# Latent attention's head linears from FP32 matmuls to three passes on split weights

## The reference

```python
def _mla_queries(a_q, q_a_norm, w_uq, q_norm, rope):
    q = (_rms_norm(a_q, q_a_norm) @ w_uq).reshape(B, L, MLA_HEADS, QK_HEAD_DIM)   # 16 heads of 96
    q = _rms_norm(q, q_norm)
    # rope on the last 32 of 96
def _mla_keys_values(a_kv, kv_a_norm, w_ukv, k_norm, rope):
    ckv = _rms_norm(a_kv[..., :KV_LORA_RANK], kv_a_norm)
    kv = (ckv @ w_ukv).reshape(B, L, MLA_HEADS, QK_NOPE_DIM + V_HEAD_DIM)         # 64 + 64
    # keys: 64 columns of kv beside 32 shared rope columns, normed, rope
```

## Time and profile before

| | |
|---|---|
| median of 3 runs | 3414.77 us (3411.88 to 3416.74) |
| span of the profiled execution | 3412.4 us; no time beside the span is recorded for it |
| TensorE busy | 3261.6 us, 96% |
| VectorE, ScalarE, GpSimd busy | 42%, 38%, 41% |
| latent attention: prologue from the first query tile to the first scores | 1044.4 to 1075.8 us |
| its 64 items, first to last scores | from 1075.8 to about 1330 us |
| items 16 to 32 by their exponentials | 1142.63 to 1216.13, 73.5 us |

### The profile page before, as it was taken

How to read it: one execution, slowest core, us unless ns; L and a number is a source line. 1 busy time by engine, 2 the same in 40 slices (tenths; PEclk the granted TensorE clock), 3 DMA queues, 4 the chain that set the end, 5 groups by cost and what they waited for, 6 DMA issues and landing times.

```text
span 3412.4 us, 40303 instructions
## 1 busy us (share of the span) xinstructions
PE 3261.6 (96%) x16296; PEld 2583.0 (76%) x16296; DVE 1418.5 (42%) x2558; ACT 1307.4 (38%) x2311; POOL 1393.8 (41%) x788
## 2 busy tenths in 40 slices
PE   7989999999999889999999999999999999999998
PEld 4864788888875456788886688888887768878887
DVE  5556342222246664321222757243232658434132
ACT  4221342212235666432333534353333443444243
POOL 2223432322343334444463036544455215554445
PEclk9989999999999999999999999999999999999999
DMA  6134223121222000423232021332323111122322
GB/s 229 62 115 180 103 86 130 56 74 45 63 83 85 13 13 10 141 84 112 84 115 99 19 79 28 104 104 84 109 86 118 51 43 60 43 90 90 108 84 71
DMA packets 85638, 286.08 MB, mean 84 GB/s; under 512 B 9771, under 2 KB 10347, under 8 KB 84940
## 3 DMA queue, kind: packets, MB, share of 16 engines
q1 hardware_dynamic: 85452, 283.50, 25.4%
HBM read 281.37 MB, written 2.10 MB: 83 GB/s over the span
## 4 chain that ended last, share of the span: by engine, by line
PE 87%; DVE 7%; ACT 4%; DMA 1%; issue 1%; POOL 0%; SPq 0%; DVEq 0%; ACTq 0%
PE ps L459 20%; PE ps L462 20%; PE ps L460 20%; PE ps L1999 2%; PE ps L499 2%; PE ps L501 2%; PE ps L500 2%; PE ps L529 1%; DMA ring<-in_w_mod 1%; PE ps L2069 1%; PE ps L1226 1%; PE ps L437 1%; PE ps L2043 1%; PE ps L2394 1%; PE ps L438 1%
## 5 line engine op out<-in xcount | busy, mean ns | idle before, releaser
L411 POOL TENSOR_TENSOR WL<-ring,WH 128x1024 fp32r<-128x1024 f32 (+2 forms) x443 | 961.4, 2174 | 1520.3 <-ACT WH L402 1519.9
L459 PE MATMUL ps<-HX,WH 128*128 128x512 f32 x1768 | 695.4, 393 | 3.0 <-POOL WL L411 3.0
L462 PE MATMUL ps<-HX,WL 128*128 128x512 f32 x1768 | 692.4, 392 | 0.0
L460 PE MATMUL ps<-HX,WH 128*128 128x512 f32 x1768 | 690.5, 391 | 0.0
L402 ACT CAST WH<-ring 128x1024 fp32r<-128x1024 f32 (+2 forms) x443 | 420.2, 950 | 371.0 <-PE ps L462 312.9
L459 PE MATMUL ps<-FR,WH 128*128 128x512 f32 x1120 | 419.1, 374 | 0.3
L460 PE MATMUL ps<-FR,WH 128*128 128x512 f32 x1120 | 409.7, 373 | 0.0
L459 PEld LDWEIGHTS ps<-HX,WH 128*128 128x128 f32 x1768 | 332.5, 188 | 82.5 <-issue 7.4
L462 PE MATMUL ps<-FR,WL 128*128 128x512 f32 x1120 | 389.4, 373 | 0.0
L462 PEld LDWEIGHTS ps<-HX,WL 128*128 128x128 f32 x1768 | 333.6, 189 | 49.9
L460 PEld LDWEIGHTS ps<-HX,WH 128*128 128x128 f32 x1768 | 332.8, 188 | 49.0
(11 more groups left out here) (391 smaller groups left out, 5096.7 us busy)
## 6 DMA issues: line engine op xcount, KB each, us to landing
ring<-in_w_mod SPq DMA_DIRECT2D x96, 512.0 KB, 5.5
ring<-in_ffn_w_up SPq DMA_DIRECT2D x88, 512.0 KB, 3.4
ring<-in_w_up SPq DMA_DIRECT2D x88, 512.0 KB, 3.3
ring<-in_w_in_tok SPq DMA_DIRECT2D x40, 512.0 KB, 3.4
ring<-in_w_in_feat SPq DMA_DIRECT2D x32, 512.0 KB, 3.3
ring<-in_ffn_w_down SPq DMA_DIRECT2D x32, 384.0 KB, 3.1
ring<-in_w_out SPq DMA_DIRECT2D x32, 384.0 KB, 3.2
ring<-in_w_down SPq DMA_DIRECT2D x32, 384.0 KB, 3.1
```

What stands on the lines that cost most here:

```text
L411: pool.tensor_tensor(WL[:, p % SPLITS, 0:n], ring.ap(r), WH[:, p % SPLITS, 0:n], ALU.subtract).then_inc(*ring.frees(r, split.g, "low", p))
L459: pe.matmul(o, high, xh, first, False)
L460: pe.matmul(o, high, xl, False, False)
L462: m = pe.matmul(PS[bs[i]][:, 0:N], low, get(k)[0], False, last)
```

## The change

The head linears join the common sequence as `L_h`, eight weights between `L_a` and `L_o`, and run in three passes. Their input gets a low part: ScalarE writes the high part in fp32r, VectorE subtracts it from the result in PSUM, and the bank is now released by VectorE. `LOW` needs room for the low parts behind the old slab, so `ARENA` grows by 1792 words; the room is taken from the scratch of dynamic transfers. ScalarE casts one weight after the last query tile and one after the last key tile of each group, three ahead in the sequence; GpSimd makes the remainders at steps 3 and 8. The three weights prepared ahead of attention are now those of group 0 and the queries of group 1, and the `L_o` weights are prepared in groups 2 and 3.

```diff
-ARENA = 27200
+ARENA = 28992
...
+        LOW = [nc.alloc_sbuf_tensor_at(f"LOW{x}", [128, 1792], F32R, offset=base + 4 * at) for x, at in enumerate((0, 27200))]
...
         L_a = Linear(ring, "mla_a").rows(dr["mla_w_a"], 0, 3, 8)
+        L_h = Linear(ring, "heads")
+        for n_ in range(4):
+            L_h.group(("q", n_), [(dr["mla_w_uq"][n_], 768, 0, 2)])
+            L_h.group(("kv", n_), [(dr["mla_w_ukv"][n_], 512, 0, 1)])
         L_o = Linear(ring, "mla_o").rows(dr["mla_w_o"], 0, 8, 8)
...
-        aq = buf(0, 2, 512)
-        ckv = buf(1024, 768)
+        aq = [x[:, 0:1024].rearrange("p (a b) -> p a b", a=2) for x in LOW]
+        ckv = [x[:, 1024:1792] for x in LOW]
...
-                    act.activation(dst, o, ACT.Identity, scale=gain).then_inc(*bank.emptied((L_a.name, g.key, s), mla.a))
+                    act.activation(low_rank_of(0, g.key, s), o, ACT.Identity, scale=gain).then_inc(
+                        *mla.a.up("rank", g.key, s))
...
+            for g in L_a.groups:
+                gain = col("mla_q_a_norm", g.key) if g.key < 2 else col("mla_kv_a_norm", 0)
+                for s in range(1 + (g.key == 2)):
+                    dve.wait_ge(*mla.a.at("rank", g.key, s))
+                    dve.scalar_tensor_tensor(low_rank_of(1, g.key, s), ps(L_a.name, g.key, s)[:, 0:(S, SC)[s]], gain,
+                                             low_rank_of(0, g.key, s), ALU.mult, ALU.subtract).then_inc(
+                        *bank.emptied((L_a.name, g.key, s), mla.v, "rank", g.key, s))
...
+        def heads_tile_pe(pe, n, what, t, x, N):
+            g = heads_of(n, what)
+            p = g.last
+            b = bank.take(what, n, t)
+            pe.wait_ge(*bank.free(what, n, t))
+            for k in range(g.kt):
+                high, low = WH[:, p % SPLITS, k * N:k * N + N], WL[:, p % SPLITS, k * N:k * N + N]
+                xh, xl = (y[:, k, t * 128:t * 128 + 128] for y in x)
+                pe.matmul(PS[b][:, 0:N], xh, high, k == 0, False)
+                pe.matmul(PS[b][:, 0:N], xh, low, False, False)
+                m = pe.matmul(PS[b][:, 0:N], xl, high, False, k == g.kt - 1)
+            m.then_inc(*(split.pe.up("used", p) if t == {"q": 3, "kv": 5}[what] else mla.pe.up(what, n, t)))
...
         def heads_pe(pe, n):
-            r = ring.raw(dr["mla_w_uq"][n], 768)
-            pe.wait_ge(*ring.landed(r))
...
+            for what, x, N, tiles in (("q", aq, 384, 4), ("kv", [y.unsqueeze(1) for y in ckv], 512, 6)):
+                p = heads_of(n, what).last
+                assert ring.next() == p
+                pe.wait_ge(*split.g.at("low", p))
...
         def heads_a(act, n):
...
                 act.copy(qtok[:, t, :], ps("q", n, t)[:, 0:384]).then_inc(*bank.emptied(("q", n, t), mla.a, "q", n, t))
+                if t == 3:
+                    cast_to(act, heads_of(n, "q").last + 3)
...
+                if t == 5:
+                    cast_to(act, heads_of(n, "kv").last + 3)
...
         def heads_g(pool, n):
             for step in range(15):
                 if step in (1, 2, 5, 6, 7):
                     square_g(pool, n, step - 1 if step < 3 else step - 3)
+                if step == 3:
+                    rest_to(pool, heads_of(n, "q").last + 3)
+                elif step == 8:
+                    rest_to(pool, heads_of(n, "kv").last + 3)
                 yield
...
-    nc = _bacc.Bacc("TRN2", target_bir_lowering=False, num_devices=1)
+    nc = _bacc.Bacc("TRN2", target_bir_lowering=False, num_devices=1, dynamic_dma_scratch_size=1024)
```

More of the change, by code:

```diff
@@ L1694, in low_rank_pe, with low_rank_of @@
             m.then_inc(*mla.pe.up("kpe"))
+        def low_rank_of(x, key, s):
+            return aq[x][:, key, :] if key < 2 else ckv[x][:, 0:512] if s == 0 else ckv[x][:, 512:768]
         def low_rank_a(act):
@@ L1703, in low_rank_a @@
                     o = ps(L_a.name, g.key, s)[:, 0:N]
-                    dst = aq[:, g.key, :] if g.key < 2 else ckv[:, 0:512] if s == 0 else ckv[:, 512:768]
                     act.activation(sq[:, g.key + s, 0:N], o, ACT.Square).then_inc(*mla.a.up())
-                    act.activation(dst, o, ACT.Identity, scale=gain).then_inc(*bank.emptied((L_a.name, g.key, s), mla.a))
+                    act.activation(low_rank_of(0, g.key, s), o, ACT.Identity, scale=gain).then_inc(
+                        *mla.a.up("rank", g.key, s))
                 mla.a.mark("low")
@@ L1797, in squares_of @@
             return s[:, 0:8 * w].rearrange("p (a b) -> p a b", a=8)
-        def heads_pe(pe, n):
-            pe.wait_ge(*mla.a.at("low"))
-            r = ring.raw(dr["mla_w_uq"][n], 768)
-            pe.wait_ge(*ring.landed(r))
[L1803 to L1828, removed]
@@ new lines, in heads_of, with done_of @@
+        def heads_of(n, what):
+            g, = (g for g in L_h.groups if g.key == (what, n))
+            return g
+        def done_of(n, what, t):
+            return split.pe.at("used", heads_of(n, what).last) if t == {"q": 3, "kv": 5}[what] else mla.pe.at(what, n, t)
+        def heads_tile_pe(pe, n, what, t, x, N):
[10 more added lines that the diff above has]
+            m.then_inc(*(split.pe.up("used", p) if t == {"q": 3, "kv": 5}[what] else mla.pe.up(what, n, t)))
@@ new lines, in heads_pe @@
+        def heads_pe(pe, n):
+            for what, x, N, tiles in (("q", aq, 384, 4), ("kv", [y.unsqueeze(1) for y in ckv], 512, 6)):
+                p = heads_of(n, what).last
+                assert ring.next() == p
+                pe.wait_ge(*split.g.at("low", p))
+                for c in range(2):
+                    pe.wait_ge(*mla.v.at("rank", *((c, 0) if what == "q" else (2, c))))
+                for t in range(tiles):
+                    heads_tile_pe(pe, n, what, t, x, N)
+                    if t % 2:
+                        yield
+                if what == "q":
+                    for _ in range(2):
+                        yield
@@ L1857, in heads_a @@
             for t in range(4):
-                act.wait_ge(*mla.pe.at("q", n, t))
+                act.wait_ge(*done_of(n, "q", t))
                 if n:
@@ L1869, in heads_a @@
             for t in range(6):
-                act.wait_ge(*mla.pe.at("kv", n, t))
+                act.wait_ge(*done_of(n, "kv", t))
                 kv = ps("kv", n, t)[:, :].rearrange("p (h c) -> p h c", h=4)
```

## The result

| | before | changed | |
|---|---|---|---|
| median of 7 runs each, alternating | 3411.88 us (3407.97 to 3416.74) | 3422.93 us (3412.22 to 3425.18) | ratio 1.0025 [1.0016, 1.0035], +8.5 us (5.5 to 12) |
| span of the profiled execution | 3412.4 us | 3421.1 us | its time was 3422.9 us |
| prologue: first head matmul to first scores | 31.3 us | 36.2 us | forecast +9.7 |
| attention: 2nd to 64th exponential | 252.9 us | 261.0 us | forecast +5.3 |

The account below looks back on a forecast made before the run. TensorE carried 87% of the chain, but in latent attention the limit moved between engines. Terms 9.0 + 0.7 - 5.0 + 4.6 + 4.2 + 1.5 gave +15.0 us: span 3427.4, median 3429.8, range 3419 to 3436.

Parts of the forecast that it names:

- passes, attention: Query and key/value tiles beside attention: single-pass matmuls shorten TensorE's part of the chain, -5.0 us.
- casts: Attention: ScalarE's weight casts stand on the chain between the last copy and the next exponential, +4.6 us.
- items 8 to 10 (remainders of step 8): Key side of attention: GpSimd's remainder holds the shared port and delays a small VectorE operation, +4.2 us.
- remainders of step 3: Query side of attention: GpSimd's remainders mostly covered by other chain work, +1.5 us, bounds 0 and 5.0.
- low-rank stage: Before the statistics: four VectorE subtractions fall in idle time; nothing, or 1 us if the cover failed.
- slot wait: Prologue: w_mod load 5 waits for q2's ring slot, freed only after GpSimd's remainder, +9.0 us.
- clock after it: Prologue, after the load wait: all 40 head transposes at the lower clock instead of about 23, +0.7 us.
- Rival 1: Prologue: the late slot is harmless, its wait and clock terms vanish; +5.3 us, 3420.1; chance 0.12.
- rival 2: Attention: GpSimd loses the port, not VectorE, so the 4.2 goes; +10.8 us, 3425.6; chance 0.13.
- scratch: Whole kernel: nothing in the trace depends on the scratch size, so no cost was forecast.
- Slower by over 0.2%: Whole kernel: slower by more than 0.2% (6.8 us), covering the forecast and two rivals; chance 0.82.
- The likeliest case: Whole kernel: the forecast itself, a median of 3425 to 3434 us; chance 0.60.

Follow-up runs that it names:

- e0: The changed kernel run again unaltered: 3419.96 us, ratio 1.0025 to the kernel before.
- e4: Changed kernel with three passes only: head weights loaded as before, not cast or split, output weights multiplied instead; 3404.69 us, ratio 0.9983 to the kernel before.
- e3: Changed kernel with GpSimd's remainders of groups 1 to 3 moved to steps 11 and 12; 3418.36 us, ratio 1.0021 to the kernel before.
- e5: Changed kernel with GpSimd's remainders in groups 1 to 3 cut to 64 columns; 3423.66 us, ratio 1.0036 to the kernel before.
- e6: Changed kernel with ScalarE's casts in groups 1 to 3 cut to 64 columns; 3421.97 us, ratio 1.0029 to the kernel before.
- e9: e3 with key/value tiles 3 and 5 of each group computed twice to keep TensorE busy; 3423.2 us, ratio 1.0041 to the kernel before.
- e1: Changed kernel with GpSimd making q2's remainder before the fifth square in group 0; 3419.42 us, ratio 1.0021 to the kernel before.
- e2: Changed kernel with each ScalarE cast one step later, behind the next exponential; 3420.55 us, ratio 1.0026 to the kernel before.
- e8: e123 with the prologue's w_mod loads asked for ahead of kv1 and q2, whose casts and remainders move later; 3409.28 us, ratio 0.9996 to the kernel before.
- e123: Changed kernel with the moves of e1, e2 and e3 together; 3408.85 us, ratio 0.9994 to the kernel before.

## Why the prediction was right in sign and half wrong in size

Terms in us, measured from the repeat (e0) and the experiments. Each is read at the items where it stands:

| term | forecast | measured | from |
|---|---|---|---|
| passes, attention | -5.0 | -4.0 | e4: -3.5, and -0.5 in item 1 |
| casts | +4.6 | +3.6 | changed less e4: +4.15, less 0.5 in items 3 and 4 |
| items 8 to 10 (remainders of step 8) | +4.2 | +4.8 | 3 x 1.6 |
| remainders of step 3 | +1.5 | +0.45 | e0 less e3: +0.18, 0 and +0.27 in the three groups |
| low-rank stage | 0 | 0 | below |
| slot wait | +9.0 | +7.0 (7.8 in the first profile) | 29.3 (30.1) against 22.3 |
| clock after it | +0.7 | -2.9 | 6.05 against 8.98 |
| sum | +15.0 | +9.0 | the stage +9.5, item 1 -0.5; median +8.3 to +8.5 |

In the first profile the same terms give +12.5: 2.7 of the fall in item 44 and 0.8 more of slot wait come on top. That this lies nearer to the forecast is luck.

**The step that failed is "Clock".** The prediction put it that "the new wait is longer and ends later, so I expect all 40 transposes at the lower level". It hung the low stretch on the end of the wait. In six executions of this prologue (the first profile, e0, e3, e5, e6, e9) none of the 40 ran at the lower level. The low stretch set in 1.3 to 4.5 us into the wait of about 12 us and was over before the first transpose: 2.7 to 4.6 us of work lay under it, against 9.3 in the kernel before, and from the last w_mod matmul to the first scores took 6.0 to 6.1 us, against 8.98. 3.6 of the 6.0 us by which the sum was off are this term. I had read only the two rows at the ends of the stretch and not where it began, and the bounds 0 to 3 left out the gain that was to come. A gain was possible because the kernel before was itself paying for a low clock there, 6.54 us for work of 4.4: a stage that already pays can be paid back. I should have put -2.1 (6.54 - 40 x 0.11) into the bounds.

Why the stretch ended when it did is not shown. It lasted 10.2 us in three of the six, in the kernel before and in e1, but 13.7 us in the other three, and 17.1 us in e2, where the wait was as long and 9.0 us of work lay under the low clock. That a longer wait uses up the low stretch describes the six executions and not e2; the gain of 2.9 us is measured, its rule isn't.

**Slot wait.** Mechanism, place and chain were right to the instruction: issue at 1065.60, forecast 1066.3; e1 shows that it hangs on the order of the remainder and the fifth square. The size was 1 to 2 us high: 8.6 us from the issue of load 7 to the end of its matmuls had been measured with all of those matmuls at the lower clock, and it took 7.5 here, where the last of them ran at the upper one (back from 1072.0 on). That is in part the clock again, priced from a stretch at the lower level. Rival 1 was half true in a way that I had not priced: VectorE's keys are there only 26 to 28 us after the first head matmul, whatever the loads do (e8), and earlier loads buy nothing below that.

**Passes.** The price of a pass was right, 0.175 against 0.172 us. A pair of query tiles gives 0.49 and 0.48 us, where 0.73 and 0.54 were forecast: the first pair of a group took 2.32 us on the chain and not 2.06, since the 0.2 us by which it had been longer than the second pair (2.79 against 2.60) stayed. Key tiles give 0.25 and 0.29 (forecast 0.2 each) in the second and third group and nothing in the first. Another 1.5 us appeared in the prologue of e4, which the forecast had counted only as a shorter way to the fifth square. The Trainium skill, "FP8 and Floating Point Precision", TensorE Precision Notes, counts four passes for true FP32; the estimate from it was 1.95 us for a pair. The rows have 12 x 0.175 = 2.1, so the row-based price was the nearer one.

**Casts.** Place right: behind the copy, in front of the exponential, 0.3 to 0.95 us each on the chain. What the forecast lacked is what follows: TensorE, made late by the last cast of a group, waits 1.6 to 1.8 us, and the clock falls in most cases. With the casts alone in their places (e3) attention is 6.9 us above passes alone, with both in theirs (e0) 8.9.

**Remainders of step 8.** The size was right (1.6 in each group, forecast 1.0, 1.6, 1.6), but in part by luck, since another cost of the same size stood in its place. In the first profile GpSimd held the port in the third group, and L2037 took 1.71 us. In the other two groups, and in all three of e0, the cast made TensorE late, the clock fell, and the late maximum met the remainder at its end or not at all (0.22 to 0.31 us). Had only the port been true, e3 would have gained 5.3 us in attention with the 0.45 of step 3; it gained 2.1. Where no long cast stands in front (e2, e6) the mechanism holds in all six groups: L2037 took 1.7 to 2.2 us and items 8 to 10 12.26 to 12.73. The rule of the Trainium skill ("SBUF — State Buffer", Who interferes with whom) agrees with these: VectorE's operation, which starts no sooner than the remainder, ends with it. In no run did a remainder of 1024 columns in attention last over 2.37 us, whether it held VectorE or not, so rival 2, in which GpSimd loses the port, is out.

**Remainders of step 3.** They did hold VectorE: L2037 took 0.89 us in item 20 and 1.97 in item 36. But item 21 gives all of it back, and item 37 1.24 of 1.51 us. An upper bound of 5.0 and a guess of 1.5 for a term whose cover was named; the cover held, but for 0.45 us.

**Low-rank stage and scratch.** The four subtractions ran at 1026.1, 1027.9 and 1035.3 (two) in VectorE's idle time, and TensorE goes from the statistics to the first head matmul with the same 1.34 us between starts as before. Nothing in the trace shows a price for the smaller scratch.

**The forecast of the median.** 3429.8 rested on a median of three runs, 3414.8; over thirty runs it is 3411.7. From that base the sum would have said 3426.7, the measured terms say 3420.7, and 3420.0 and 3422.9 were measured. "Slower by over 0.2%" came true at 0.25%. The likeliest case (3425 to 3434) did not: the time fell between rivals 1 and 2, for neither's reason.

**A better version.** e123 beats the changed kernel (3408.9 against 3420.0) and equals the kernel before within its interval, -2.3 us with the upper end at +0.7. Passes alone save 5.8, so with its parts in place the change may be worth 2 us, which this measurement can't tell from nothing. What remains is the prologue: VectorE's keys, and the low clock behind the waits there.

## What to carry to other kernels

When preparation work is added beside a chain, its place in each engine's program costs more than its length: here the same casts and remainders cost 9 us of attention in one place and 0.1 us one to eight steps later. Two delays in one item may replace each other instead of adding up, so undo them together before you judge either, and read periods, not totals. Before pricing a load that is moved ahead of others in an in-order queue, follow its slot to the instruction that releases it; and of a stretch at the low clock read where it begins as well as where it ends, since what lies in it is what you pay for, and read it in more than one execution.

## What the runs showed of the hardware that was not expected

- A wait of TensorE of 1.6 to 1.9 us inside dense work was followed, 19 times in 25, by 3.4 or 6.8 us at a granted clock of 0.50. Such a fall cost 1.6 us in items 8 to 10 (e5), and 0.6 to 2.7 us in items 12, 28 and 44.
- In the prologue the granted clock fell 1.2 to 5.0 us after the start of TensorE's wait for loads or keys and stayed at 0.50 for 3.4 us (e123), 6.8 (e4, e8), 10.2 (before, changed, e0, e1, e9), 13.7 (e3, e5, e6) or 17.1 us (e2), with one and the same program in the changed kernel, e0, e5 and e6. What decides on the length was not settled.
- A GpSimd subtraction of 128x1024 (2.36 us) held a VectorE operation on one column for 1.7 to 2.2 us, to its own end. Where TensorE was late by as much (e0) it cost nothing more, and in item 45 of e3 nothing at all.
- A single-pass matmul of 384 columns starts 0.17 to 0.18 us before the next at the upper level; one of 512 0.22 to 0.23.
